# Hybrid decoder block on one core: modulation product moved to TensorE, state-space quarters and indexer blocks woven in another order

## The chip, the cores and the metric

One core of a Trainium2 chip runs the whole kernel in one launch. The metric is the device time in microseconds (us), and lower is better. Engines are named as in the profile: PE is TensorE, PEld its weight loads, DVE VectorE, ACT ScalarE, POOL GpSimd, SPq the queue of DMA issues on SyncE and ACTq that on ScalarE.

## The reference

One layer on 512 tokens of width 1024, all float32:

```python
ada = silu(c) @ w_ada + b_ada                       # 1024 -> 6144: shift1, scale1, gate1, shift2, scale2, gate2
u = rms_norm(h, norm1_g) * (1 + scale1) + shift1
u_ssm, q, k, v, q_idx, k_idx, w_idx, g_ssm, g_attn = split(u @ w_in)
y_ssm  = s5_mixer(u_ssm)                            # 32 groups, state 64, complex diagonal scan, GLU
y_attn = dsa_attention(q, k, v, q_idx, k_idx, w_idx)
mixed = sigmoid(g_ssm) * (y_ssm @ w_proj_ssm) + sigmoid(g_attn) * (y_attn @ w_proj_attn)
h = h + gate1 * (mixed @ w_out)
u2 = rms_norm(h, norm2_g) * (1 + scale2) + shift2
h = h + gate2 * moe_ffn(u2)                         # 64 experts, top 8, and a shared one
out = rms_norm(h, norm_f)
# dsa_attention, per block of 128 queries:
score = sum over 8 heads of w_idx * relu(q_idx @ k_idx.T); sel = top_k(causal(score), 128)
p = softmax(q @ k[sel].T / 8 - slope * distance); y = p @ v[sel]
```

## The kernel before, in words

Each engine runs a program written out by hand, and semaphores tie them together. PSUM results ("groups") go to banks in the order of the list `groups_in_order()`: a group takes bank `ORDER[g] % NB`, and PE waits until the group `NB` places earlier was copied out, by DVE for the kinds in `BY_VECTOR` and else by ACT. Weights stream through three slots of 2 MB in the order of `stream_items()`; SyncE issues them in that order, each when the item three places earlier is no longer used, so one late item holds all behind it. The items ("A", n) are the twelve 2 MB pieces of `w_ada`; four pieces make one part of 2048 outputs.

The stages, in order of time:

- Start. `ada_piece(0)` to `(3)` on DVE multiply and add a piece into the 128-partition accumulator `ADA` (L1069, two instructions of 128x2048 a piece). Between the pieces DVE makes the norm's factor. PE transposes the scaled rows of x (`uT`, L1501) and sums `ADA` over the partitions (`mod`, L1608), and DVE and ACT scale `uT` by the result (L1104, L900). Only then can `ssm`, the first projection, start.
- Projections `ssm`, `kkT`, `vwT`, `qiT` on PE (L1521), with small transposes `cT` between them.
- State space and indexer. The 32 groups of the state space are worked in four quarters q. POOL builds the tables of a quarter (`s5_tables(q)`: BA, then CA, then W2; L591, L666, L673, L684). `s5_build(q)` on PE makes bT and K of BA and CA, DVE's `s5_kernel(q)` makes a Toeplitz kernel of K. `s5_apply(q)` on PE: u chunks (`uc`), v1 and v2 (L1572, L1578), a gate projection `gs`, and y (L1591 to L1593), for which DVE must have ended `s5_scan(q)` (L1121 to L1134) and POOL W2(q). `s5_phases(q)` on DVE makes the next scan's angles. The key indexer of block i: eight head products `idx` (256, 384 and 512 keys wide for i = 1, 2, 3), a relu copy by ACT into two buffers in turn, and a multiply-add over the heads by DVE (`index_scores(i)`, L1153). `top_k(i)` on DVE takes the 8 largest 16 times (L1161, L1162).
- Projection `qT`, then four attention blocks i of 8 heads: logits (PE), bias and maximum (DVE, L1225 to L1227), exp (ACT), transpose and product with v (PE). Eight gate projections stand in them at the places `FILL`. `top_k(3)` stands in blocks 0 and 1, `top_k(2)` ahead of block 0, and half a piece of `w_ada` on DVE two heads behind each of the eight fills.
- GLU, the sums of `ADA` over the partitions (`ada`, n = 4 to 11), branches, output projection, routing and 43 passes of the experts. Their code is the same in both kernels.

## Time and profile before

| | |
|---|---|
| runs of the kernel before | 1324.74, 1328.32, 1328.75 us; median 1328.32 |
| the profiled execution | 1327.42 us, its span 1325.7 us |
| first projection starts | 53.40 us |
| projection qT starts | 265.51 us |
| first logits of attention block 1, 2, 3 | 326.8, 356.9, 391.8 us |
| attention ends on PE | 426.3 us |

The engines' shares of the whole span (PE 88%, DVE 43%, POOL 20%) are averages over stages with different limits, so the table gives the borders of the stages that the change touches. Everything behind 426 us waits for what comes before it in one chain.

### The profile page before, as it was taken

To read this page: it belongs to the slowest core of one execution; us is meant where nothing else is said; L and a number is where in the kernel's file an instruction comes from. 1 tells how busy PE (TensorE), PEld (TensorE's weight loads), DVE (VectorE), ACT (ScalarE), POOL (GpSimd) and SP (SyncE) were. 2 spreads that over 40 slices of the span, in tenths; PEclk is the share of its full clock that TensorE was granted. 3 is DMA by queue.
4 is the path that set the end of the run, shared out by engine and by line. 5 is a ranking of instruction groups with operands and counts; after the bars stand their busy time and mean duration, and the time that the engine had idled before them with its cause. 6 is when DMAs were issued, how large, how long until landed. Compare 5 with 4: busy or idle time off the path is not lost. (4 is left out here: it accounts for less than half of the span.)

```text
span 1325.7 us, 13190 instructions
## 1 busy us (share of the span) xinstructions
PE 1166.0 (88%) x4654; PEld 569.8 (43%) x4655; DVE 566.9 (43%) x1175; ACT 226.8 (17%) x449; POOL 260.1 (20%) x250
## 2 busy tenths in 40 slices
PE   0799677797999999989789999999998999999854
PEld 0544455544555444444433444444444444444321
DVE  5325989877744412343722232222222222232138
ACT  2411231123324000111001111111111111111111
POOL 7852478200000000001001111111111111111100
PEclk9799787898899999999889999999999999999977
DMA  8726100331213212220969999999999899899776
GB/s 324 187 87 206 26 9 10 97 147 84 109 83 140 83 64 79 80 83 6 376 262 347 422 419 394 362 379 416 385 413 421 339 383 401 344 420 376 268 315 264
DMA packets 84902, 318.37 MB, mean 240 GB/s; under 512 B 29842, under 2 KB 32914, under 8 KB 56162
## 3 DMA queue, kind: packets, MB, share of 16 engines
q1 hardware_dynamic: 64084, 277.96, 53.6%
q0 software_dynamic: 14352, 36.23, 7.2%
q10 hardware_dynamic: 6400, 3.33, 1.1%
q8 instruction: 38, 0.62, 0.2%
q14 instruction: 28, 0.23, 0.0%
HBM read 302.14 MB, written 29.89 MB: 250 GB/s over the span
## 5 line engine op out<-in xcount | busy, mean ns | idle before, releaser
L1521 PE MATMUL ps<-uTs,ring 128*128 128x512 f32 (+2 forms) x496 | 228.4, 619 | 3.3 <-DMA ring<-in_w_in 2.6
L1789 PE MATMUL ps<-ring,XT 128*128 128x512 f32 x416 | 183.0, 593 | 0.4 <-ACT XT L998 0.4
L1822 PE MATMUL ps<-ring,XT 128*64 128x512 f32 (+1 forms) x800 | 148.8, 595 | 0.9 <-ACT XT L998 0.9
L1521 PEld LDWEIGHTS ps<-uTs,ring 128*128 128x128 f32 (+2 forms) x496 | 95.6, 196 | 122.7 <-issue 118.2
L1383 DVE TENSOR_TENSOR uTs<-uTs,ps 128x256 f32<-128x256 f32 x47 | 19.8, 421 | 283.5 <-ACT uTs L1002 283.5
L738 POOL DMA_INDIRECT XT<-u_rows,idx x48 | 49.0, 1021 | 409.0 <-DVE idx L1372 387.0
L1789 PEld LDWEIGHTS ps<-ring,XT 128*128 128x128 f32 x416 | 77.2, 191 | 87.8 <-issue 87.2
L1833 PE MATMUL ps<-ring,uTs 128*128 128x512 f32 x208 | 98.8, 619 | 3.2 <-DMA ring<-in_w_exp_down 3.1
L1424 DVE TENSOR_SCALAR uTs<-ps,gat 128x512 f32<-128x512 f32 x47 | 35.3, 751 | 128.3 <-PE ps L1833 70.1
L1822 PEld LDWEIGHTS ps<-ring,XT 128*64 128x64 f32 (+1 forms) x800 | 46.4, 128 | 87.4 <-issue 84.1
L1852 PE MATMUL ps<-ring,uTs 128*64 128x512 f32 (+1 forms) x400 | 80.2, 626 | 1.8 <-DMA ring<-in_w_exp_down 1.7
L1501 PEld LDWEIGHTS ps<-ident,XT 128*128 128x128 f32 x424 | 53.1, 189 | 53.3 <-DMA XT<-u_rows,idx 38.6
L1501 PE MATMUL ps<-ident,XT 128*128 128x128 f32 x424 | 60.6, 288 | 16.5 <-DMA XT<-u_rows,idx 10.3
L744 POOL DMA_INDIRECT expert_rows<-uTs,adx x47 | 47.5, 1011 | 139.7 <-DVE uTs L1424 139.7
L591 POOL TENSOR_TENSOR ring<-ring 128x512 f32<-128x512 f32 (+4 forms) x35 | 56.9, 1625 | 79.0 <-issue 28.0
L1069 DVE SCALAR_TENSOR_TENSOR ADA<-ring,sm,ADA 128x2048 f32<-128x2048 f32 x24 | 60.1, 2506 | 27.9 <-DMA ring<-in_w_ada 14.2
L1002 ACT ACTIVATE uTs<-ps 128x256 f32<-128x256 f32 x47 | 18.1, 384 | 310.2 <-PE ps L1789 169.9
L712 POOL DMA_DIRECT2D u_rows<-XT x4 | 2.4, 612 | 326.9 <-DVE XT L1266 326.9
L1007 ACT ACTIVATE uTs<-ps,gat 128x512 f32<-128x512 f32 x47 | 32.3, 688 | 162.6 <-PE ps L1833 87.7
L1833 PEld LDWEIGHTS ps<-ring,uTs 128*128 128x128 f32 x208 | 38.4, 195 | 42.5 <-issue 42.2
L1521 PE MATMUL ps<-ring,UB 128*128 128x512 f32 x128 | 55.4, 593 | 1.5 <-DVE UB L1253 1.5
L836 ACT ACTIVATE ring<-ps 128x512 f32<-128x512 f32 (+3 forms) x60 | 29.5, 505 | 117.1 <-PE ps L1521 106.6
(319 smaller groups left out, 1377.9 us busy)
## 6 DMA issues: line engine op xcount, KB each, us to landing
ring<-in_w_exp_gate SPq DMA_DIRECT2D x64, 1024.0 KB, 10.5
ring<-in_w_exp_up SPq DMA_DIRECT2D x64, 1024.0 KB, 15.0
ring<-in_w_exp_down SPq DMA_DIRECT2D x64, 1024.0 KB, 14.7
ring<-in_w_ada SPq DMA_DIRECT2D x12, 2048.0 KB, 12.2
ring<-in_w_in SPq DMA_DIRECT2D x7, 2048.0 KB, 9.0
ring<-expert_rows SPq DMA_DIRECT2D x6, 2048.0 KB, 18.6
ring<-in_w_out SPq DMA_DIRECT2D x2, 2048.0 KB, 8.7
H<-in_x SPq DMA_DIRECT2D x1, 2048.0 KB, 14.1
```

The costliest lines, as they stand in the source:

```text
L591: link(E.tensor_tensor(o, x, y, op))
L738: E.indirect_dma_start(xg[par], None, U2D, bass.IndirectOffsetOnAxis(idx[:, col:col + 1], 0), bounds_check=SEQ - 1, oob_is_err=False).then ...
L744: E.indirect_dma_start(YD, bass.IndirectOffsetOnAxis(adx[:, col:col + 1], 0), y, None, bounds_check=SEQ * EK - 1, oob_is_err=False).then_i ...
L1007: A(ye[p % 2][:, 512:1024], ps[7][:, :], ACT.Copy, scale=gat[:, p % RING:p % RING + 1]).then_inc(S["y_out_s"], 1)
L1069: return V.scalar_tensor_tensor(acc, a3(arrived(dve, ("A", n)), 2)[:, k], csil[:, 2 * j + k:2 * j + k + 1], acc, ALU.mult, ALU.add)
L1424: V.tensor_scalar(ye[p % 2][:, 0:512], ps[6][:, :], gat[:, p % RING:p % RING + 1], None, ALU.mult)\
L1501: return nc.tensor.transpose(o, i, ident[0:k, 0:k])
L1521: ins = mm(b[0:rows_, 0:cols], l, r, start=(k == 0), stop=(k == len(chunks) - 1))
L1789: ins = mm(a3(ps[0][:, :], 2), xgT[par][:, k], wgu[r][:, k], start=(k == 0), stop=(k == KD - 1))
L1822: ins = mm(a3(ps[0][c, :], 2), xgT[par][:, k, c], wgu[r][:, k], start=(k == 0), stop=(k == KD - 1))
L1833: ins = mm(ps[6 + n][:, :], hTe[:, k], a3(wdn[r], 2)[:, k, 512 * n:512 * (n + 1)], start=(k == 0), stop=(k == 1))
L1852: ins = mm(ps[6 + n][c, :], hTe[:, k, c], a3(wdn[r], 2)[:, k, 512 * n:512 * (n + 1)], start=(k == 0), stop=(k == 1))
```

## The change

1. `w_ada` on PE: `ada_piece(n)` takes a column of silu(c), repeated to 32 columns, as the weights, and writes four quarters of 512 outputs to the four groups of 32 partitions of bank 5, which it keeps (`NB` is 5). `ada_row(part)` on DVE adds the bias once a part. The `mod` product becomes four transposes, and `ada` picks its row with a column of the identity. x is loaded ahead of `w_ada`.
2. `s5_build(0)`, `uc` of quarter 0 stand among the `qiT` projections; quarter 0 is applied ahead of every indexer block; then indexer block i stands ahead of `s5_apply(i)`, i = 1, 2, 3, and `s5_build(q + 1)` inside `s5_apply(q)`.
3. `top_k(1)` stands behind the last scan, `top_k(2)` in attention block 0 and `top_k(3)` in block 1, two rounds a head.

```diff
@@ -44,7 +44,7 @@
-NB = 6
+NB = 5
...
-        return [("uc", q), ("v1", q), ("v2", q), ("gs", q)] + [("y", q, n) for n in range(2)]
+        return [("v1", q), ("v2", q), ("gs", q)] + (s5_build(q + 1) if q + 1 < NQ else []) + [("y", q, n) for n in range(2)]
+
+    def indexer(i):
+        return [("idx", i, h) for h in range(NH - 2)] + [("uc", i)] + [("idx", i, h) for h in range(NH - 2, NH)]
-    o += [("kkT", 0), ("vwT", 0), ("vw", 0)] + [("qiT", m) for m in range(4)]
-    o += [("idx", 1, h) for h in range(NH)] + s5_build(0)
-    o += [("idx", 2, h) for h in range(NH)] + s5_apply(0) + s5_build(1)
-    o += [("idx", 3, h) for h in range(NH)] + s5_apply(1) + s5_build(2)
-    o += s5_apply(2) + s5_build(3) + s5_apply(3)
+    o += [("kkT", 0), ("vwT", 0), ("vw", 0), ("qiT", 0), ("qiT", 1)] + s5_build(0)
+    o += [("qiT", 2), ("uc", 0), ("qiT", 3)] + s5_apply(0)
+    for i in range(1, TT):
+        o += indexer(i) + s5_apply(i)
...
+        ada_rows = [ADA[:, 2048:2560], ADA[:, 4096:4608], ADA[:, 4608:5120]]
...
+            sp.dma_start(H[:], a["x"][0].rearrange("(t p) d -> p t d", p=P)).then_inc(S["x_in"], 16)
+
+            def bias_of_part(part):
+                for q in range(4):
+                    c0 = 2048 * part + 512 * q
+                    sp.dma_start(ada_rows[part][32 * q:32 * (q + 1), :], a["b_ada"][0:1, c0:c0 + 512].broadcast_to((32, 512)))\
+                        .then_inc(b_in[part], 16)
+
             load(("A", 0))
-            sp.dma_start(H[:], a["x"][0].rearrange("(t p) d -> p t d", p=P)).then_inc(S["x_in"], 16)
             load(("A", 1))
-            for n, c in enumerate((slice(0, 2 * DM), slice(2 * DM, 6 * DM))):
-                sp.wait_ge(S["ada_zero"], n + 1)
-                sp.dma_start(ADA[0:1, c], a["b_ada"][0:1, c]).then_inc(b_in[n], 16)
+            bias_of_part(0)
             for g in list(ITEMS)[2:]:
                 if g == ("misc", 0):
                     state_tables()
-                if g == ("A", 5):
+                    bias_of_part(1)
+                    bias_of_part(2)
+                if g == ("gs", 0):
...
+            s5_tables(2)
             causal(1)
+            s5_tables(3)
             causal(2)
-            s5_tables(2)
             causal(3)
-            s5_tables(3)
...
+                    if h == NH - 2:
+                        chunks(i)
...
-            for m in range(4):
+            for m in range(2):
                 out_copy(("qiT", m), qiT[:, m, :])
             phases(0)
-            indexer(1)
             arrange_u(0)
             s5_build(0)
-            indexer(2)
+            out_copy(("qiT", 2), qiT[:, 2, :])
+            chunks(0)
+            out_copy(("qiT", 3), qiT[:, 3, :])
             s5_apply(0)
-            phases(1)
-            s5_build(1)
-            indexer(3)
-            s5_apply(1)
-            phases(2)
-            s5_build(2)
-            s5_apply(2)
-            phases(3)
-            s5_build(3)
-            s5_apply(3)
+            for q in range(1, NQ):
+                phases(q)
+                indexer(q)
+                s5_apply(q)
...
-            V.memset(ADA[:, 0:2 * DM], 0.0).then_inc(S["ada_zero"], 1)
-            V.memset(ADA[:, 2 * DM:6 * DM], 0.0).then_inc(S["ada_zero"], 1)
-
-            dve.wait_ge(b_in[0], 16)
-            dve.wait_ge(S["c_silu"], 1)
-
-            def ada_half(n, k):
-                part, j = n // 4, n % 4
-                acc = ADA[:, 2048 * part:2048 * (part + 1)]
-                return V.scalar_tensor_tensor(acc, a3(arrived(dve, ("A", n)), 2)[:, k], csil[:, 2 * j + k:2 * j + k + 1], acc,
-                                              ALU.mult, ALU.add)
-
-            def ada_piece(n):
-                link(ada_half(n, 0))
-                signal(ada_half(n, 1), "ada_sum", n + 1)
+            def ada_row(part):
+
+                dve.wait_ge(b_in[part], 64)
+                dve.wait_ge(S["ada_sum"], 4 * (part + 1))
+                V.tensor_tensor(ada_rows[part], ada_rows[part], ps[5][:, :], ALU.add).then_inc(S["ada_row"], 1)
...
-            for n in range(2):
-                ada_piece(n)
             dve.wait_ge(S["squares"], 1)
             rms_scale(slice(0, TT), 1)
             V.tensor_copy(junk1, rstd[:, 0:1]).then_inc(S["rstd_ok"], 1)
-            for n in range(2, 4):
-                ada_piece(n)
+            ada_row(0)
...
-            dve.wait_ge(b_in[1], 16)
             dve.wait_ge(S["scan_zero"], 1)
-            ada_piece(4)
             taken(dve, ("vw", 0))
             link(V.tensor_scalar(wis, vw[:, :, HD:HD + NH], float(NH * 64) ** -0.5, None, ALU.mult))
             s5_phases(0)
-            ada_piece(5)
-            index_scores(1)
             s5_kernel(0)
-            index_scores(2)
-            s5_scan(0)
-            s5_phases(1)
-            s5_kernel(1)
-            index_scores(3)
-            s5_scan(1)
-            s5_phases(2)
-            s5_kernel(2)
-            ada_piece(6)
-            s5_scan(2)
-            s5_phases(3)
-            top_k(1, 0, 4)
-            s5_kernel(3)
-            top_k(1, 4, 10)
-            s5_scan(3)
-            top_k(1, 10, 16)
-            ada_piece(7)
-            top_k(2, 0, 16)
+            for q in range(NQ):
+                s5_scan(q)
+                if q + 1 < NQ:
+                    s5_phases(q + 1)
+                    s5_kernel(q + 1)
+                    index_scores(q + 1)
+            top_k(1, 0, 16)
+            ada_row(1)
...
-                        top_k(3, n, n + 1)
+                    if i < 2:
+                        top_k(2 + i, 2 * h, 2 * h + 2)
...
-                    if (i, h - 2) in FILL:
-                        k = list(FILL).index((i, h - 2))
-                        if k % 2 == 0:
-                            link(ada_half(8 + k // 2, 0))
-                        else:
-                            signal(ada_half(8 + k // 2, 1), "ada_sum", 9 + k // 2)
...
+            ada_row(2)
             for n in range(4, 12):
+                if n == 9:
+                    done(dve, ("ada", 11))
                 ada_out(n)
...
+            def ada_piece(n):
+
+                part, j = n // 4, n % 4
+                w = a3(arrived(pe, ("A", n)), 2)
+                if n == 0:
+                    pe.wait_ge(S["c_silu"], 1)
+                elif j == 0:
+                    pe.wait_ge(S["ada_row"], part)
+                for k in range(2):
+                    col = csil[:, 2 * j + k:2 * j + k + 1].broadcast_to((P, 32))
+                    for q in range(4):
+                        ins = mm(ps[5][32 * q:32 * (q + 1), :], col, w[:, k, 512 * q:512 * (q + 1)],
+                                 start=(j == 0 and k == 0), stop=(j == 3 and k == 1))
+                ins.then_inc(S["ada_sum"], 1)
+
             def ada(n):
-                pe.wait_ge(S["ada_sum"], 4 * (n // 4 + 1))
-                end(product(("ada", n), [(ones[:], ADA[:, 512 * n:512 * (n + 1)])]))
+                pe.wait_ge(S["ada_row"], n // 4 + 1)
+                row = ident[:, 32 * (n % 4):32 * (n % 4) + 1].broadcast_to((P, P))
+                end(product(("ada", n), [(row, ada_rows[n // 4])]))
...
+            def s5_apply(q):
+                if 1 <= q < 3:
+                    ada_piece(4 + q)
...
+                if q + 1 < NQ:
+                    s5_build(q + 1)
...
                 for h in range(NH):
+                    if h == NH - 2:
+                        chunks(i)
...
+            ada_piece(0)
+            ada_piece(1)
             for t in range(TT):
                 pe.wait_ge(S["u_tile"], t + 1)
                 transposed_rows("uT", t, ut4)
-            pe.wait_ge(S["ada_sum"], 4)
+            ada_piece(2)
+            ada_piece(3)
+            pe.wait_ge(S["ada_row"], 1)
             b = begin(("mod", 0))
-            for c in range(2 * KD):
-                ins = mm(b[:, c:c + 1], ADA[:, P * c:P * (c + 1)], ones[:, 0:1], start=True, stop=True)
+            for c in range(4):
+                ins = tr(b[:, P * c:P * (c + 1)], ada_rows[0][:, P * c:P * (c + 1)])
...
-            pe.wait_ge(S["u_ok_v"], KD // 2)
-            pe.wait_ge(S["u_ok_s"], KD // 2)
             w = a3(arrived(pe, ("ssm", 0)), 8)
             for t in range(TT):
-                end(product(("ssm", t), [(uT[:, k, P * t:P * (t + 1)], w[:, k]) for k in range(KD)]))
+                b = begin(("ssm", t))
+                for k in range(KD):
+                    if t == 0:
+                        pe.wait_ge(S["u_ok_s" if k % 2 else "u_ok_v"], k // 2 + 1)
+                    ins = mm(b[:, :], uT[:, k, P * t:P * (t + 1)], w[:, k], start=(k == 0), stop=(k == KD - 1))
+                end(ins)
...
-            for m in range(4):
+            for m in range(2):
                 projection_t("qiT", m, w, P * m)
-            taken(pe, ("qiT", 3))
+            s5_build(0)
+            projection_t("qiT", 2, w, P * 2)
+            chunks(0)
+            projection_t("qiT", 3, w, P * 3)
...
-            indexer(1)
-            s5_build(0)
-            indexer(2)
+            ada_piece(4)
             s5_apply(0)
-            s5_build(1)
-            indexer(3)
-            s5_apply(1)
-            s5_build(2)
-            s5_apply(2)
-            s5_build(3)
-            s5_apply(3)
+            taken(pe, ("qiT", 3))
+            for q in range(1, NQ):
+                indexer(q)
+                s5_apply(q)
             w = a3(arrived(pe, ("q", 0)), 8)
             for m in range(4):
                 projection_t("qT", m, w, P * m)
+            ada_piece(7)
...
+                        if list(FILL).index((i, h)) % 2:
+                            ada_piece(8 + list(FILL).index((i, h)) // 2)
```

On ACT the helper `chunks(q)` (the copy of `uc` and the arranging of the next quarter's chunks) is cut out of `s5_apply` in the same way.

PE at the start, before: the transposes of the rows of x (`UB`), the product `mod` and the first projection.

```order
L1501 MATMUL ps<-ident,K16s 128x32 x2
L1501 MATMUL ps<-ident,UB 128x128 x32
L1608 MATMUL ps<-ones,ADA 128x1 x16
L1521 MATMUL ps<-ring,uTs 128x512 x32
L1501 MATMUL ps<-ident,XT 128x128 x8
```

The same place after (`ring,sm 32x512` is a piece of `w_ada`, 8 products each):

```order
L1482 MATMUL ps<-ident,K16s 128x32 x2
L1521 MATMUL ps<-ring,sm 32x512 x16
L1482 MATMUL ps<-ident,UB 128x128 x32
L1521 MATMUL ps<-ring,sm 32x512 x16
L1482 MATMUL ps<-ident,ADA 128x128 x4
L1625 MATMUL ps<-ring,uTs 128x512 x32
```

Two pieces now stand on each side of the transposes, and four transposes in the place of sixteen products.

DVE from the last angle of quarter 0 to its scan, before (`score` rows are the indexer's, `ADA` a piece of `w_ada`, `K16s` the Toeplitz kernel, L1121 the scan's first instruction):

```order
L1069 SCALAR_TENSOR_TENSOR ADA<-ring,sm,ADA 128x2048 x2
L1151 TENSOR_SCALAR score<-GB,sm 128x256
L1153 SCALAR_TENSOR_TENSOR score<-GB,sm,score 128x256 x7
L1111 TENSOR_TENSOR sm<-ident,sm 16x128
L1115 COPY K16s<-ps 16x4x112
L1116 TENSOR_TENSOR K16s<-ps,sm 16x4x16
L1115 COPY K16s<-ps 16x4x112
L1116 TENSOR_TENSOR K16s<-ps,sm 16x4x16
L1151 TENSOR_SCALAR score<-GB,sm 128x384
L1153 SCALAR_TENSOR_TENSOR score<-GB,sm,score 128x384 x7
L1121 TENSOR_SCALAR ring<-ring,sm 128x512
```

DVE after, from the kernel of quarter 1 to its scan:

```order
L1109 TENSOR_TENSOR sm<-ident,sm 16x128
L1113 COPY K16s<-ps 16x4x112
L1114 TENSOR_TENSOR K16s<-ps,sm 16x4x16
L1113 COPY K16s<-ps 16x4x112
L1114 TENSOR_TENSOR K16s<-ps,sm 16x4x16
L1149 TENSOR_SCALAR score<-GB,sm 128x256
L1151 SCALAR_TENSOR_TENSOR score<-GB,sm,score 128x256 x7
L1119 TENSOR_SCALAR ring<-ring,sm 128x512
```

Two indexer blocks stood ahead of the scan of quarter 0; now the first of them stands between the kernel of quarter 1 and its scan.

DVE in attention block 0, before (one head; `score` 128x512 is a round of `top_k(3)`):

```order
L1161 MAX sm<-score 128x8
L1162 MATCH_REPLACE score<-sm,score 128x512
L1225 SCALAR_TENSOR_TENSOR ring<-ps,ring 128x128
L1226 TENSOR_REDUCE sm<-ring 128x1
L1227 TENSOR_SCALAR sm<-sm 128x1
```

After, ahead of the same head:

```order
L1159 MAX sm<-score 128x8
L1160 MATCH_REPLACE score<-sm,score 128x384
L1159 MAX sm<-score 128x8
L1160 MATCH_REPLACE score<-sm,score 128x384
L1209 SCALAR_TENSOR_TENSOR ring<-ps,ring 128x128
```

A head carries two rounds in the place of one, 384 wide in block 0 and 512 wide in block 1.

## Rows read from the trace of the kernel before

**Rows 1.** Engines by stretch: us, busy time with (x instructions), PE clock, DMA share, GB/s

```profile
0.00:53.40 53.40, 13.34 (x67) 12.95 (x68) 28.90 (x25) 24.27 (x37) 38.15 (x58) 0.89 0.81 261
53.40:127.20 73.80, 73.12 (x172) 31.61 (x172) 24.77 (x27) 7.55 (x13) 36.98 (x26) 0.96 0.48 151
127.20:265.50 138.30, 101.19 (x625) 73.51 (x624) 123.37 (x172) 34.20 (x85) 78.11 (x53) 0.83 0.16 46
...
295.00:326.80 31.80, 23.93 (x80) 12.73 (x78) 23.84 (x56) 13.11 (x34) 0.00 (x0) 0.84 0.31 129
326.80:356.90 30.10, 27.56 (x102) 15.21 (x101) 23.80 (x51) 8.77 (x27) 0.00 (x0) 0.89 0.06 14
356.90:391.80 34.90, 33.28 (x127) 19.46 (x126) 16.39 (x30) 10.82 (x27) 0.00 (x0) 0.85 0.42 170
391.80:426.30 34.50, 32.72 (x150) 19.32 (x149) 17.60 (x29) 13.52 (x28) 0.00 (x0) 1.00 0.23 84
```

**Rows 2.** Timeline of DVE and PE at the start: start, us, what [idle before]

```profile
20.62 10.37 DVE L1069 SCALAR_TENSOR_TENSOR ADA<-ring,sm,ADA 128x2048 f32<-128x2048 f32 x4 [13.28 <-DMA ADA<-in_b_ada]
...
32.73 10.00 DVE L1069 SCALAR_TENSOR_TENSOR ADA<-ring,sm,ADA 128x2048 f32<-128x2048 f32 x4
...
42.79 6.99 PE L1608 MATMUL ps<-ones,ADA 128*128 128x1 f32 x32 [2.78 <-DVE ADA L1069]
53.40 30.57 PE L1521 MATMUL ps<-ring,uTs 128*128 128x512 f32 x64 [3.62 <-issue]
```

**Rows 3.** Loads: SyncE issues, first use of x, GB/s in 40 slices of 0 to 40 us

```profile
7.65 18.54 SPq L424 DMA_DIRECT2D ring<-in_w_ada  x2
...
15.80 1.06 ACT L825 ACTIVATE UB<-H 128x1024 f32<-128x1024 f32 x1 [4.01 <-DMA H<-in_x]
...
GB/s 0 10 109 270 394 385 409 426 274 139 346 394 410 426 426 422 402 393 410 394 402 418 418 443 328 25 82 197 393 434 401 434 281 348 410 406 408 378 153 28
```

**Rows 4.** Timeline of DVE, index_scores(1), (2) and (3) without their first instruction

```profile
129.68 3.61 DVE L1153 SCALAR_TENSOR_TENSOR score<-GB,sm,score 128x256 f32<-128x256 f32 x7
...
136.97 13.22 DVE L1153 SCALAR_TENSOR_TENSOR score<-GB,sm,score 128x384 f32<-128x384 f32 x7
...
172.60 12.33 DVE L1153 SCALAR_TENSOR_TENSOR score<-GB,sm,score 128x512 f32<-128x512 f32 x7
```

**Rows 5.** As rows 1: W2(1); BA, CA(2); scans 1, 2, 3; y(1); v1 to y(0) with build(1); build(0)

```profile
167.70:175.20 7.50, 6.29 (x42) 3.60 (x40) 5.09 (x7) 4.18 (x8) 7.14 (x5) 1.00 0.00 0
176.60:194.70 18.10, 13.74 (x64) 8.73 (x64) 17.75 (x13) 3.18 (x5) 17.37 (x11) 0.72 0.12 17
184.90:195.20 10.30, 9.87 (x48) 4.88 (x44) 10.05 (x11) 0.40 (x1) 9.31 (x7) 0.81 0.12 17
213.50:226.80 13.30, 8.49 (x20) 3.46 (x16) 13.05 (x10) 0.60 (x1) 12.83 (x7) 0.88 0.06 9
251.70:257.30 5.60, 4.70 (x11) 1.72 (x10) 5.35 (x11) 0.60 (x1) 0.00 (x0) 1.00 0.11 17
195.20:200.70 5.50, 5.43 (x49) 5.26 (x49) 5.19 (x11) 0.96 (x5) 0.00 (x0) 1.00 0.00 0
...
148.30:169.60 21.30, 21.22 (x136) 15.98 (x136) 15.79 (x28) 5.03 (x14) 4.45 (x4) 0.85 0.10 15
130.20:133.10 2.90, 2.90 (x27) 2.30 (x26) 2.72 (x6) 2.35 (x6) 0.00 (x0) 1.00 1.01 429
```

**Rows 6.** Timeline: SyncE issues w_in of q behind the last gs; PE begins qT

```profile
256.43 0.37 SPq L427 DMA_DIRECT2D ring<-in_w_in  x1
...
265.51 27.73 PE L1521 MATMUL ps<-uTs,ring 128*128 128x512 f32 x64 [2.63 <-DMA ring<-in_w_in]
```

**Rows 7.** Groups by form: busy us, mean ns | idle before; 32-column tiles, rounds of top_k(3)

```profile
L1852 PE MATMUL ps<-ring,uTs 128*32 128x512 f32 x128 | 16.3, 653 | 0.1
...
L1161 DVE MAX8 sm<-score 128x8 f32<-128x512 f32 x16 | 11.0, 686 | 0.1
L1162 DVE MATCH_REPLACE8 score<-sm,score 128x512 f32<-128x512 f32 x16 | 10.8, 676 | 0.0
```

19 lines of the change are left out of this document (11 added, 8 removed).

## The prediction, made before the changed kernel ran

> **What bounds the kernel now.** I read the engines by stretch first [rows 1]. Behind 426 us both kernels run the same code in one chain, so I take a microsecond saved or lost ahead of that point as a microsecond of the whole. Ahead of it the stages have different limits. From 0 to 53.4 us PE is busy 13.3 us: it waits for the modulation. From 53.4 to 127.2 it is busy 73.1 of 73.8, so the projections are PE's. From 127.2 to 265.5 PE has 101 of 138 us and DVE 123 of 138: DVE's order of work bounds the state space. In attention blocks 0 and 1 PE and DVE share the bound (24 and 24 of 31.8 us; 28 and 24 of 30.1), and blocks 2 and 3 are almost PE's (33.3 of 34.9, 32.7 of 34.5).
>
> At the start DVE first touches a piece of w_ada at 20.6 us, held by the bias row, and has 20.4 us of such work ahead of mod, which costs PE another 7.0; the first projection follows at 53.4 [rows 2]. The loads are no limit there for long: the GB/s row adds up to 2.1, 4.2, 6.3 and 8.4 MB at about 8, 14.5, 20 and 25 us and then falls to 25 GB/s, because SyncE issues the fourth piece only when DVE has used the first, at 26.2 us (7.65 + 18.54) [rows 3].
>
> In the state space index_scores costs 0.52 us an instruction (3.61 / 7) while GpSimd rests, but 1.89 and 1.76 us (13.22 / 7, 12.33 / 7) while it builds tables [rows 4]. A scan takes 10.3 and 13.3 us beside tables and 5.6 without [rows 5]. So the two engines slow each other down, or rather DVE pays, and where a block stands against the tables matters more than its length.
>
> **Term 1, the start.** Removed from the path: DVE's 20.4 us and mod's 7.0. x is now the first load, so it lands near 9 us and not at the 15.8 of [rows 3], and norm and transposes hide behind the pieces. PE takes piece 0 at about 15 and frees its slot by 17, while loads are still queued; the dip at 25 us goes. At 410 GB/s, with 0.3 MB of bias, piece 3 is in by 31 and the weights of ssm by 36. A piece on PE is 8 float32 products of two instructions on 32 columns. The nearest row has 128 such instructions in 16.3 us, 0.127 us each [rows 7], so 16 make 2.0 us, and up to 4.0 at half clock. Piece 3 ends at 34, the bias add and four transposes take an estimated 1.5, and of the 3.6 us between mod's end and the first projection (42.79 + 6.99 to 53.40 [rows 2]) I keep 1.5, as PE now waits chunk by chunk. T0, the start of ssm, is 37: a gain of 16.4, from 12 (the norm's gain vector or the angles late) to 18.
>
> The Trainium skill, TensorEngine Tiling (Array Packing), section Key Properties, lets tiles work in parallel but says that changing the tiling mode drains the engine. That speaks against pieces of 2 us strewn among full-width products. The row above comes from passes that stand between full-width products, so it already holds such changes, and I add nothing for it.
>
> **Term 2, from T0 to qT.** Before: 265.5 - 53.4 = 212.1. After, in PE's order: the projections 73.8 [rows 1], build(0) 2.9, uc an estimated 0.7, piece 4 2.0, then v1, v2, gs, build(1) and y(0), which are the 21.3 us of [rows 5]: y(0) ends at T0 + 100.7. DVE's scan 0 hides beside gs, since GpSimd rests then. Three quarters follow.
> - Quarter 1. GpSimd starts with W2(1), 7.5, when y(0) is out, then BA and CA of quarter 2, 18.1 [rows 5], which build(2) needs; with K (an estimated 1.9) and y(1), 5.5, that makes 33.0. DVE's way is as long: 2 until the first relu, eight instructions, scan 12, y 5.5. The block is 256 wide, and its own row says 0.52; beside tables I take 1.6, from the 1.76 and 1.89, so 12.8 and together 32.3. I take 33.
> - Quarter 2. DVE works without a pause: phases and kernel 9.6 (11 of the 13 phases' instructions take 5.2 [rows 5]), index 15 (8 x 1.89), scan 12 (between 10.3 and 13.3). I take 36.6.
> - Quarter 3. Only W2(3) is left, so about three of the eight instructions are slow. uc is out 12 us behind y(2), v1, v2 and gs take 12.5, and q's weights arrive 9.1 us behind gs (265.51 - 256.43 [rows 6]): 33.6.
>
> Pieces 5 and 6, 2.0 each, stand where PE waits for DVE; without that cover they would cost 4. SyncE issues eight bias loads more ahead of misc, which is needed a whole ssm (30.57 us [rows 2]) later, and the chunk loads now ahead of gs: nothing.
>
> Sum: 100.7 + 33 + 36.6 + 33.6 = 203.9, a gain of 8.2. Bounds: GpSimd's 33.0 holds in quarters 1 and 2 even if DVE were quick, so the gain is at most 14 here; with 1.89 everywhere and scans of 13.3 it falls to 2, and a stall of a few us a quarter makes it a loss of 4. Against the 256 row alone quarter 1 would be no shorter, but phases(2) would start earlier: 2.4 us more gain.
>
> The Trainium skill, GPSIMD Engine Reference, section Key points, says that GpSimd shares its SBUF interfaces with VectorE and contends with its instructions of two SBUF inputs. By that the 256 block, moved from a rest of GpSimd into its tables, becomes slow, and top_k, moved out, gains nothing; the 384 and 512 rows agree, and no row here shows the 256 block under tables.
>
> **Term 3, attention.** top_k(1) stands beside qT (27.7 us of PE) and is hidden there. Piece 7 behind qT meets ACT's table loads and gelu; bounds 0 and 2, I take 1. A round of top_k on 512 keys is 0.686 + 0.676 and the small load and gaps, 1.5 us [rows 7]; on 384 an estimated 1.25. Block 0: eight rounds of 512 (12) become sixteen of 384 (20), and two halves of a piece leave (2 x 2.3 estimated): DVE goes from 23.8 to 27.2 us of 31.8, and PE with piece 8 from 23.9 to 26. It fits, as DVE can run two heads ahead inside a fill: 0. Block 1: sixteen rounds of 512 for eight, less two halves, is 23.8 + 12 - 4.7 = 31.1 us in a block of 30.1. If all its waits vanish it costs 1, if they stay (6.3) it costs 7.3; walking the heads through the two fills gives 3.7, which I take. Blocks 2 and 3 are PE's: pieces 10 and 11 cost 2.0 each. Sum: a loss of 8.7, from 4 to 14.
>
> **Term 4, behind GLU.** ada_row(2) comes after DVE's product with the gate, just when PE reaches the sums of the third part: a loss of 1, from 0 to 3. Five banks in the place of six: a projection lasts 6.9 us and its copy well under 1, so I put it at nothing in the projections, and inside the walk above in attention.
>
> **Sum.** -16.4 - 8.2 + 8.7 + 1 = -14.9. The profiled execution took 1327.4 us, of which 1325.7 are its span; the median of the runs is 0.9 above it. 1327.4 - 14.9 + 0.9 gives 1313 us.
>
> **Rivals.**
> - Less contention (0.12): tables and DVE miss each other, term 2 gains 14 and block 1 costs 1. For it: GpSimd is idle 60 of the stage's 138 us [rows 1]. Against: the index block now starts just when W2 does. 1304 or a little under.
> - Attention bounded by DVE (0.12): block 1 pays 7.3 and block 0 some 4, as the fills leave DVE without logits. 1321.
> - Loads late at the start (0.06): piece 3 or the small loads behind 10 MB land 6 us later. For it: the bias row, issued at 3 us, held DVE until 20.6. 1319.
> - The new order stalls (0.07): a relu buffer holds uc, uc holds v1 and ca_ok holds build by turns, 5 to 6 us a quarter. Term 2 becomes a loss of about 8: 1329, no difference to slightly slower.
> - Slower (0.05): the four tiles of a piece don't overlap, so a piece costs 16 x 0.433 = 6.9 us (27.73 / 64 [rows 6]). Each of the five pieces 7 to 11 then costs 4.9 more on PE, in blocks with no room: +25, 1338. It ends the gain when a piece takes about 5 us. Against it stands the 0.127 of [rows 7], whose moving data is the same shape.
>
> **How the numbers follow.** The forecast holds 0.58, with its own range 1305 to 1320. From 1300 to 1326 lie it, the first three rivals and some of the fourth. A measurement of this kernel tells about 0.3%, 4 us, from no change, so faster means under 1324: 0.58 + 0.12 + 0.12 + 0.05 = 0.87, from which I take 0.01 for the tails. Within 4 us 0.07, slower 0.07.
>
> **What would show it.** Piece products near 2 us; ssm at 35 to 40 us, and no dip in the GB/s at 25; y(0) about 101 us behind ssm; W2(1) starting with y(0)'s copy and the 256 block at about 1.6 us an instruction; qT near 241; block 0 as long as before, block 1 about 4 longer, 2 and 3 about 2 longer; the same time behind attention. I am wrong if PE's first projection is still held past 45 us, if a quarter takes over 40 us, or if block 1 passes 38.

## The result, and the profile after

The changed kernel took 1318.57 us (median of 8 runs, 1314.11 to 1322.73) against 1327.06 us before (8 runs, 1324.74 to 1329.89). The ratio is 0.9936, with a 95% interval of 0.992 to 0.9953: 8.5 us faster, where 14 were forecast. The execution that was profiled is the quickest of the eight (1314.11 us, span 1312.4). From the start of the output projection on (522.42 us after, 531.40 before), where both kernels run the same code, it takes 4.3 us less than the one before; at that border it is 9.0 us ahead, and this is the part that answers to the medians.

Engines by stretch, the changed kernel: us, busy time with (x instructions) of PE, PEld, DVE, ACT, POOL, then PE clock, DMA share, GB/s. The borders are the first projection, the end of y(0), the starts of index blocks 2 and 3 (one quarter each), qT, the first logits of blocks 0 to 3, GLU and the output projection.

```profile
0.00:38.59 38.59, 16.86 (x102) 7.32 (x103) 4.25 (x16) 24.09 (x37) 22.43 (x52) 0.98 0.93 338
38.59:138.99 100.40, 96.88 (x356) 48.24 (x357) 28.76 (x56) 15.38 (x29) 51.34 (x42) 0.97 0.50 152
138.99:172.60 33.61, 28.31 (x177) 17.85 (x176) 30.36 (x32) 8.39 (x23) 22.99 (x15) 0.85 0.07 9
172.60:206.70 34.10, 28.68 (x178) 18.41 (x176) 30.85 (x36) 9.12 (x23) 24.66 (x16) 0.90 0.06 9
206.70:238.72 32.02, 25.44 (x138) 16.61 (x136) 28.10 (x60) 8.95 (x24) 10.32 (x12) 0.84 0.29 88
238.72:271.84 33.12, 33.12 (x112) 15.17 (x113) 5.19 (x16) 5.54 (x6) 0.31 (x1) 0.95 0.38 142
271.84:305.34 33.50, 27.29 (x92) 13.39 (x90) 26.48 (x78) 11.25 (x33) 0.00 (x0) 0.85 0.24 99
305.34:340.81 35.47, 29.33 (x118) 15.50 (x117) 29.23 (x70) 8.88 (x27) 0.00 (x0) 0.90 0.10 31
340.81:378.00 37.19, 35.54 (x141) 19.68 (x140) 11.77 (x28) 10.81 (x27) 0.00 (x0) 0.86 0.35 141
378.00:416.26 38.26, 36.48 (x166) 20.51 (x165) 13.09 (x27) 13.47 (x28) 0.00 (x0) 0.96 0.27 95
416.26:522.42 106.16, 104.19 (x246) 45.60 (x246) 27.18 (x39) 9.53 (x12) 0.00 (x0) 1.00 0.23 80
```

Blocks 0 to 3 answer to the last four rows of [rows 1]. qT was this row of the same view in the kernel before:

```profile
265.51:295.08 29.57, 29.57 (x95) 13.98 (x95) 23.40 (x50) 3.58 (x5) 0.21 (x1) 1.00 0.32 116
```

Taken together, stretch by stretch:

| stretch | before | after | difference | forecast |
|---|---|---|---|---|
| start to the first projection | 53.40 | 38.59 | -14.8 | -16.4 |
| first projection to qT | 212.1 | 200.1 | -12.0 | -8.2 |
| qT to the end of attention | 160.75 | 177.54 | +16.8 | +8.7 |
| GLU to the output projection | 105.1 | 106.2 | +1.0 | +1.0 |
| sum | | | -9.0 | -14.9 |

Timeline of PE at the start: start, us, what, and in brackets the idle time before it with what ended it. It answers to [rows 2].

```profile
15.54 3.64 PE L1521 MATMUL ps<-ring,sm 128*32 128x512 f32 x16 [6.85 <-DMA ring<-in_w_ada]
20.99 3.64 PE L1521 MATMUL ps<-ring,sm 128*32 128x512 f32 x16 [1.81 <-DMA ring<-in_w_ada]
...
29.32 1.92 PE L1521 MATMUL ps<-ring,sm 128*32 128x512 f32 x16
32.05 1.92 PE L1521 MATMUL ps<-ring,sm 128*32 128x512 f32 x16 [0.81 <-DMA ring<-in_w_ada]
34.86 0.66 PE L1482 MATMUL ps<-ident,ADA 128*128 128x128 f32 x4 [0.89 <-DVE ADA L1074]
38.59 21.80 PE L1625 MATMUL ps<-ring,uTs 128*128 128x512 f32 x44 [3.07 <-DMA ring<-in_w_in]
```

A piece takes 3.64 us at the lower clock and 1.92 at the full one, and each of the idle times but one ends with a load (DMA share 0.93 in the first stretch).

Timeline of PE in attention block 1, the changed kernel:

```profile
307.93 0.44 PE L1482 MATMUL ps<-ident,ring 128*128 128x128 f32 x2 [1.46 <-ACT ring L954]
311.93 0.69 PE L1482 MATMUL ps<-ident,ring 128*128 128x128 f32 x2 [2.94 <-ACT ring L954]
312.42 9.32 PE L1502 MATMUL ps<-uTs,ring 128*128 128x512 f32 x16
...
329.09 0.44 PE L1482 MATMUL ps<-ident,ring 128*128 128x128 f32 x2 [1.74 <-ACT ring L954]
```

Before the two fills, 2.94 and 1.74 us of idle stand where there were 0.66 and 0.22: ACT's exp is named, but it waits for DVE's maximum, and that stands behind two rounds of the selection. Three things went into the 16.8 us. PE's idle time (length less busy) is 15.8 us for 13.8, so 2.0 more. The time at half clock, (1 - clock) x 2 x length in each row, is 33.9 us for 27.3. It costs something only where PE is busy, and half of its length there: read in steps of 0.25 us, PE was busy in 31.1 of the 33.9 us and in 22.2 of the 27.3 (in block 0 of the kernel before, 3.4 us of it fell on idle PE). That makes 4.5 us. Five pieces of 2.05 us each, a price that e4 takes apart, make 10.2. Together that is 16.7.

### The profile page after: what moved, and what is told of

Its sections match the earlier page's. It is cut to its first block and busy times, and to the rows that moved or that the text cites. A ratio compares the mean times of both kernels' runs of the same rounds, so it can differ in the third digit from the quotient of the medians.

```text
span 1312.4 us, 13490 instructions
## 1 busy us (share of the span) xinstructions
PE 1186.5 (90%) x4818; PEld 561.9 (43%) x4819; DVE 493.8 (38%) x1152; ACT 226.9 (17%) x449; POOL 238.5 (18%) x250
## 5 line engine op out<-in xcount | busy, mean ns | idle before, releaser
L1502 PE MATMUL ps<-uTs,ring 128*128 128x512 f32 (+2 forms) x496 | 234.0, 631 | 3.1 <-DMA ring<-in_w_in 2.5
L1364 DVE TENSOR_TENSOR uTs<-uTs,ps 128x256 f32<-128x256 f32 x47 | 19.8, 421 | 284.9 <-ACT uTs L1012 284.9
L1482 PEld LDWEIGHTS ps<-ident,XT 128*128 128x128 f32 x424 | 52.9, 189 | 49.1 <-DMA XT<-u_rows,idx 36.6
L601 POOL TENSOR_TENSOR ring<-ring 128x512 f32<-128x512 f32 (+4 forms) x35 | 48.7, 1391 | 73.1 <-ACT UB L899 40.3
L1502 PE MATMUL ps<-XT,ring 128*128 128x512 f32 x96 | 42.7, 593 | 0.0
## 6 DMA issues: line engine op xcount, KB each, us to landing
ring<-in_w_exp_gate SPq DMA_DIRECT2D x64, 1024.0 KB, 10.7
```

The source lines that it names most:

```text
L601: link(E.tensor_tensor(o, x, y, op))
L1482: return nc.tensor.transpose(o, i, ident[0:k, 0:k])
L1502: ins = mm(b[0:rows_, 0:cols], l, r, start=(k == 0), stop=(k == len(chunks) - 1))
```

## Experiments

Theory A, at the start of the study: some 8 of attention's 16.8 us come from the selections in blocks 0 and 1 (waits, and the lower clock behind waits), and the rest from pieces that cost 1.92 us each where PE is the bound. Rival B: the loss is the pieces, the fifth bank and the clock, whatever DVE does.

**e1: selections beside qT again**

```diff
             top_k(1, 0, 16)
+            top_k(2, 0, 16)
             ada_row(1)
...
                     if i < 2:
-                        top_k(2 + i, 2 * h, 2 * h + 2)
+                        top_k(3, n, n + 1)
```

> The changed kernel with one thing undone: the selection for query block 2 (16 rounds) stands beside the q projection again, behind that for block 1, and attention blocks 0 and 1 hold one round a head of block 3's selection. Theory A: of the 16.7 us that the stretch from the q projection to the end of attention lost, the selections in blocks 0 and 1 made some 8: the waits for VectorE and, behind them, fills at the lower clock. Then block 1 falls from 35.5 to about 32, the stretch ahead of block 1 from 37.3 to about 35, and the kernel is 5 to 9 us quicker than the changed one (about 1312). Theory B: the loss is the pieces' own time on TensorE, the fifth bank and the clock, whatever VectorE does. Then the kernel stays within 2 us of the changed one (about 1318).

It took 1307.70 us (1306.81 to 1309.17; ratio to before 0.9864, interval 0.985 to 0.9879): 10.9 us less than the changed kernel (9.9 if each is set against the kernel before of its own session, 1326.09 and 1327.06), somewhat over A's range. Engines by stretch, qT and blocks 0 to 3:

```profile
240.04:273.29 33.25, 33.25 (x113) 15.12 (x113) 23.26 (x61) 5.55 (x6) 0.03 (x1) 0.95 0.37 139
273.29:304.21 30.92, 25.71 (x92) 12.84 (x90) 17.68 (x51) 11.17 (x33) 0.00 (x0) 0.89 0.26 107
304.21:337.07 32.86, 29.76 (x117) 15.64 (x116) 19.09 (x49) 8.88 (x27) 0.00 (x0) 0.90 0.10 33
337.07:369.42 32.35, 30.71 (x142) 17.09 (x141) 11.71 (x28) 10.70 (x27) 0.00 (x0) 1.00 0.40 163
369.42:407.67 38.25, 36.47 (x166) 20.52 (x165) 13.09 (x27) 13.47 (x28) 0.00 (x0) 0.96 0.27 97
```

DVE's 18 us of selection vanish beside qT (its busy time there goes from 5.2 to 23.3 us, the stretch stays at 33). The attention is 9.9 us shorter: 2.6 in each of blocks 0 and 1, and 4.8 in block 2, where no selection was. Block 2 has the same instructions and the same idle time as in the changed kernel, but a clock of 1.00 for 0.86. The rival is out: the selections in blocks 0 and 1 cost the kernel some 10 us by the medians. By the profiles 5.2 of them stand in those two blocks; whether the 4.8 of block 2 come from the selections is not shown (see the part on the prediction).

**e2: part 1 alone.** The kernel before with all of part 1 (pieces on PE, x first, five banks) and nothing of parts 2 and 3. Cut to the places of pieces 4 to 6; piece 7 stands behind qT, 8 to 11 in attention as in the changed kernel.

```diff
             def s5_apply(q):
+                if 1 <= q < 3:
+                    ada_piece(4 + q)
...
                 projection_t("qiT", m, w, P * m)
+            ada_piece(4)
```

> The kernel before with the modulation product on TensorE alone (x loaded first, five banks, bias by parts), with the old order of the state space and the old places of the selections; pieces 4 to 7 stand on TensorE before the index blocks, ahead of uc of quarters 1 and 2, and behind the q projection. Theory A: the start gives 14.8, and VectorE, relieved of pieces 4 to 7 (some 4.7 us each) and bound in the state space, gives 8 to 12 more ahead of the q projection even in the old order; attention loses some 5 to 8 for the pieces. Sum about 1327 - 14.8 - 10 + 6 = 1308. Theory B: the gain of 12.0 ahead of the q projection comes from the new order of quarters and index blocks. Then this kernel gains the start alone and pays attention's pieces: about 1327 - 14.8 + 6 = 1318.

1318.41 us (1317.37 to 1321.26; ratio 0.9949, 0.9936 to 0.9963), the time of the whole change. The first projection starts at 39.21, qT at 247.69: ahead of qT 208.5 us, a gain of 3.6, not A's 8 to 12. Attention takes 169.9 us, 9.1 more than before. Theory B of this run holds. With e1 the three parts come apart. Each median is set against the kernel before of its own session: e2 -7.7, e1 -18.4, the changed kernel -8.5.

| step | kernels | us |
|---|---|---|
| part 1, product on PE | e2 less before | -7.7 |
| part 2, new order of quarters and index blocks | e1 less e2 | -10.7 |
| part 3, selections into attention | changed less e1 | +9.9 |

The third part gave back what the second had brought. By the profiles, 4.9 of the 10.7 us and 4.8 of the 9.9 stand in block 2 of attention (37.25 us in e2, 32.35 in e1, 37.19 in the changed kernel) and go with its clock.

**e3 and e7: why a piece takes 1.92 us**

```diff
-                for k in range(2):
-                    for q in range(4):
+                for q in range(4):
+                    for k in range(2):
```

> The changed kernel with the two loops of a piece exchanged: both products of one group of 32 output rows follow each other, then those of the next group, so neighbours mostly write the same rows. If products on different 32-column groups run beside each other only when they are neighbours, most of the overlap goes: a piece takes from 1.92 us up to 5 to 6.9 us (16 x 0.433), the four in attention and piece 7 cost 3 to 4.9 us more each, the start some 5 more: 1338 to 1350. If the short time of a piece does not come from that overlap, a piece stays near 1.9 us and the time within 2 us of the changed kernel.

1318.39 us (1316.56 to 1320.94), pieces of 1.94 us: the order in which the four groups are written makes no difference. This left two explanations, and e7 tells them apart (pieces n with n % 4 > 0 write only the first 32 rows, so the modulation's values are wrong, the count of products is the same; the flags that open and close the sums are set to match):

```diff
-                        ins = mm(ps[5][32 * q:32 * (q + 1), :], col, ...)
+                        r = q if j == 0 else 0
+                        ins = mm(ps[5][32 * r:32 * (r + 1), :], col, ...)
```

> The changed kernel with all eight products of pieces 1 to 3, 5 to 7 and 9 to 11 sent to the first group of 32 output rows (the modulation is then wrong in value; same count and shape of products). Theory A: a piece takes 1.92 us because products on four groups run beside each other, each group with its own queue deep enough that their order in the program doesn't matter. On one group they can't: a piece takes 6.9 us (16 x 0.433), five of pieces 7 and 9 to 11 and those at the start cost some 5 us each: 1338 to 1348. Theory B: a product on 32 columns is short by itself (0.12 us), with or without neighbours: 1318, a piece 1.9 us.

Timeline of PE in block 1 of e7:

```profile
350.53 7.05 PE L1522 MATMUL ps<-ring,sm 128*32 128x512 f32 x16
```

7.05 us for 16 instructions on one group: a product on 32 columns is as long as a full one, and the 1.92 us are four groups at work beside each other. The price of the forecast's rival (6.9 us a piece) was right, its condition wasn't met. Attention is 15.7 us longer than in the changed kernel and the start 13.0. The whole, 1418.19 us, can't be compared: other modulation chooses other experts.

The Trainium skill, TensorEngine Tiling (Array Packing), section Key Properties, says that tiles run their matrix products in parallel, and these two runs agree. It names no condition on their order; of the two orders tried within 16 instructions, both overlap.

**e4: pieces 8 to 11 all but out** (one product of 32 columns in the place of eight; the modulation's third part is incomplete).

```diff
-                    for q in range(4):
+                    for q in range(4 if n < 8 else 0):
...
+                if n >= 8:
+                    ins = mm(ps[5][0:32, 0:32], col, w[:, 0, 0:32], start=(j == 0), stop=(j == 3))
```

> The changed kernel with pieces 8 to 11, the four that stand in attention, cut from eight products to one of 32 columns each (the third part of the modulation is then incomplete). Theory A: TensorE is the bound in blocks 2 and 3 and ahead of block 1, so these pieces cost their 1.92 us there; in block 1 about half: 6 to 8 us quicker in all, about 1311.5. Theory B: behind the waits for VectorE a piece of TensorE is free, and the loss is waits and clock: 0 to 3 us quicker.

1305.97 us (1305.16 to 1309.83), 12.6 less than the changed kernel, more than either theory gave. Behind attention the two profiles take the same 896 us, so the incomplete modulation doesn't disturb the comparison. Engines by stretch, blocks 2 and 3:

```profile
341.80:372.47 30.67, 29.03 (x127) 16.81 (x126) 11.71 (x28) 10.70 (x27) 0.00 (x0) 1.00 0.48 194
372.47:407.36 34.89, 33.11 (x152) 19.39 (x151) 13.09 (x27) 13.47 (x28) 0.00 (x0) 1.00 0.24 87
```

Block 3 now has the clock of 1.00 that it had before, and takes 34.89 us where it took 34.51: the tiny product on 32 columns costs nearly 0.4. Timeline of PE in block 3, from its second fill to the logits behind it: the kernel before, e4, and the changed kernel.

```profile
409.91 7.03 PE L1521 MATMUL ps<-uTs,ring 128*128 128x512 f32 x16
...
417.71 1.12 PE L1521 MATMUL ps<-kT,XT 64*128 64x512 f32 x2
```

```profile
390.63 7.03 PE L1502 MATMUL ps<-uTs,ring 128*128 128x512 f32 x16
397.59 0.25 PE L1525 MATMUL ps<-ring,sm 128*32 128x32 f32 x2
...
398.80 1.12 PE L1502 MATMUL ps<-kT,XT 64*128 64x512 f32 x2
```

```profile
397.85 7.03 PE L1502 MATMUL ps<-uTs,ring 128*128 128x512 f32 x16
...
407.70 1.12 PE L1502 MATMUL ps<-kT,XT 64*128 64x512 f32 x2
```

From start to start that is 7.80, 8.17 and 9.85 us. The tiny product itself takes 0.18 to the next instruction (397.59 to 397.77), so the two changes of shape, from full width to 32 columns and back, cost 0.2 us, and a whole piece costs 9.85 - 7.80 = 2.05 us, close to the 2.0 of the forecast. The Trainium skill, TensorEngine Tiling (Array Packing), section Key Properties, has changes of the tiling mode drain the engine; a price like this would fit, but nothing here measures the drain by itself. The block's 38.26 us are then 34.51 + 2.05 + 1.7, the last for its 3.4 us at half clock (the first fill takes 8.35 us and not 7.03). In block 2 e4 is at full clock and the changed kernel isn't: 6.5 us between them, though e4 keeps the selections in blocks 0 and 1.

**e5: pieces where PE waits anyway.** e1, with pieces 8, 9 and 11 ahead of the wait for the block's first weights.

```diff
                     n = NH * i + h
+                    if h == 0 and i != 2:
+                        ada_piece({0: 8, 1: 9, 3: 11}[i])
                     pe.wait_ge(S["prob"], n + 1)
...
-                        if list(FILL).index((i, h)) % 2:
-                            ada_piece(8 + list(FILL).index((i, h)) // 2)
+                        if (i, h) == (2, 5):
+                            ada_piece(10)
```

> The kernel of e1 with pieces 8, 9 and 11 moved from behind the second fill of attention blocks 0, 1 and 3 to the head of the block, ahead of the wait for the first weights of the block (2.30, 1.46 and 1.78 us of idle TensorE in e1). Theory A: a piece costs its 1.92 us only where TensorE has no wait to lay it in, and part of what it adds is a spell at half clock. Then the three pieces cost under 1 us each: 4 to 7 us quicker than e1, about 1302; block 3 falls from 38.3 to about 35. Theory B: the place doesn't matter, since the wait moves behind the piece or the piece delays the block's own chain: within 2 us of e1 (1307.7).

1297.18 us (1293.34 to 1302.68; ratio to before 0.978, 0.9756 to 0.9804), 10.5 less than e1 and over A's range. Engines by stretch, blocks 0 to 3 of e5 (qT, 33.12 us at a clock of 0.95, is as in e1):

```profile
271.81:300.25 28.44, 24.41 (x91) 12.14 (x89) 17.68 (x51) 11.06 (x33) 0.00 (x0) 0.94 0.28 116
300.25:328.52 28.27, 26.74 (x118) 14.57 (x117) 19.10 (x49) 8.77 (x27) 0.00 (x0) 1.00 0.05 14
328.52:360.86 32.34, 30.70 (x141) 17.09 (x140) 11.70 (x28) 10.70 (x27) 0.00 (x0) 1.00 0.46 184
360.86:395.38 34.52, 34.52 (x166) 19.76 (x165) 13.09 (x27) 13.47 (x28) 0.00 (x0) 1.00 0.24 85
```

The profiled execution is e5's quickest (1293.34 us). The same work as e1 on PE, 10.9 us shorter in attention: idle time 7.2 us for 11.7, and 6.7 us at half clock for 19.8, which at half price is 6.5; both sum to 11.1. Block 3 is the plainest, and 34.52 us in all three kernels with piece 11 at its head (e5, e9, e12). In e1 PE waited 1.78 us and then ran its fill at the lower clock; in e5 the piece stands in the wait, no idle time is left in the block and the fill takes 7.03 us:

```profile
373.18 1.07 PE L1483 MATMUL ps<-ident,ring 128*128 128x128 f32 x4 [1.78 <-ACT ring L954]
374.04 8.35 PE L1503 MATMUL ps<-uTs,ring 128*128 128x512 f32 x16
```

```profile
362.77 1.92 PE L1522 MATMUL ps<-ring,sm 128*32 128x512 f32 x16
365.12 7.03 PE L1503 MATMUL ps<-uTs,ring 128*128 128x512 f32 x16
```

The first fence is e1, the second e5.

**e12: the same places, selections left in attention.** The changed kernel with e5's edit.

> The changed kernel, selections left in attention blocks 0 and 1, with pieces 8, 9 and 11 at the heads of blocks 0, 1 and 3. Theory A: the pieces' price (their time and the spells at half clock behind the waits at the heads) and VectorE's waits inside blocks 0 and 1 are apart: 8 to 10 us quicker than the changed kernel, about 1309.5, block 3 at 34.5 and block 1 still with its waits of 2.9 and 1.7. Theory B: with VectorE behind, the piece at the head of blocks 0 and 1 is no gain; only block 3's 3.7 us come: about 1314.5.

1312.35 us (1307.62 to 1315.38; ratio 0.9893, 0.9877 to 0.991), 6.2 less than the changed kernel and between the two theories. Engines by stretch, blocks 0, 1 and 3:

```profile
272.66:304.51 31.85, 27.06 (x91) 13.20 (x90) 26.48 (x78) 11.18 (x33) 0.00 (x0) 0.84 0.25 103
304.51:339.71 35.20, 30.13 (x117) 15.74 (x116) 29.24 (x70) 8.65 (x27) 0.00 (x0) 0.90 0.04 12
...
376.59:411.11 34.52, 34.52 (x166) 19.75 (x165) 13.10 (x27) 13.47 (x28) 0.00 (x0) 1.00 0.23 84
```

Block 3 gives its 3.7 us, block 0 gives 1.7, block 1 next to nothing (35.20 for 35.47; its waits ahead of the fills are 2.62 and 2.25 us for 2.94 and 1.74): while DVE sets its length, a piece laid into one wait comes back in another.

**e6, e9: GpSimd's order.** e1 with W2(q) behind BA and CA of q + 1; e9 is e5 with the same.

```diff
...
             s5_tables(0)
+            s5_w2(0)
             s5_tables(1)
             s5_tables(2)
+            s5_w2(1)
             causal(1)
             s5_tables(3)
+            s5_w2(2)
+            s5_w2(3)
             causal(2)
```

> The kernel of e1 with one thing moved on GpSimd: W2(q) (7.5 us) behind BA and CA of quarter q+1 and not ahead of them. Theory A: GpSimd's 33 us from one y to the next bound quarters 1 and 2, because build(q+1) waits 3.96 and 2.88 us for CA. With W2 behind, the table comes 7.5 us earlier and W2 is first needed by y: its floor is 25.6 + 5.5 = 31.1 us. Then the waits for CA go, the two quarters take 31 to 32.5 us instead of 33.7 and 34.1, and the kernel is 2 to 4 us quicker than e1, about 1304.5. Theory B: VectorE's row of phases, kernel, index scores and scan bounds the quarters and the wait for CA only covers for it: within 1 us of e1.

1305.83 us (1300.25 to 1307.69), 1.9 less than e1. Timeline of PE, changed kernel, the waits for CA (POOL L683), of which e6 has none:

```profile
164.14 3.21 PE L1555 MATMUL ps<-ring 128*16 128x128 f32 x16 [3.96 <-POOL ring L683]
...
199.56 1.92 PE L1555 MATMUL ps<-XT,ring 128*16 128x128 f32 x16 [2.88 <-POOL XT L683]
```

And e6 by quarters:

```profile
138.60:172.20 33.60, 28.93 (x178) 18.47 (x177) 29.57 (x32) 8.27 (x23) 23.88 (x16) 0.85 0.07 10
172.20:206.30 34.10, 30.08 (x178) 18.73 (x177) 31.56 (x36) 9.13 (x23) 24.25 (x15) 0.85 0.06 9
```

The waits are gone, and the two quarters (33.6 and 34.1 us, DVE busy 29.6 and 31.6 of them) are as long as in the changed kernel: the wait for CA had mostly covered one for DVE. So far B holds, but not to the end. In e1 itself the two quarters took 32.4 and 36.6, and seven kernels with the same code ahead of qT, but for the order of the loads in e8 and within a piece in e3 (the changed one, e1, e3, e4, e5, e8, e12) need 200.1 to 202.6 us from the first projection to qT. e6 needs 199.2 and e9 199.5. The new order of GpSimd may thus be worth about 1 us, less than A said; such a difference is within the scatter of these kernels and not shown.

> e5 and e6 together: selection for block 2 beside the q projection, pieces 8, 9 and 11 at block heads, W2(q) behind BA and CA of q+1. Theory A: e5 took 10.5 us from e1 in attention and e6 1.9 ahead of it, in different stretches, so they add: about 1295.5. Theory B: e6's 1.9 us is the scatter of the state space from kernel to kernel (from y(0) to y(3) 96 to 100 us among kernels with the same order there): the same as e5, 1297.

1293.77 us (1288.97 to 1300.9; ratio 0.9756, 0.9731 to 0.9781): the fastest version, 32.4 us less than the kernel before in the same session (1326.12). That it beats e5 is not certain, since the two intervals overlap. Its profiled execution needs 199.5 us from the first projection to qT, e5's 200.1. In attention the two have the same code and agree in blocks 1 to 3, but block 0 took 32.59 us at a clock of 0.79 in e9 and 28.44 at 0.94 in e5: a piece at the head of that block doesn't always spare it the lower clock.

**e10, e11: VectorE relieved, meant to be.** Seven of eight index score instructions of a block on 64 keys (the scores are incomplete); e10 is the changed kernel with this, e11 is e6.

```diff
-V.scalar_tensor_tensor(sc_of[i], relu[:, n % 2, 0:w], wcol, sc_of[i], ALU.mult, ALU.add)
+V.scalar_tensor_tensor(sc_of[i][:, 0:64], relu[:, n % 2, 0:64], wcol, sc_of[i][:, 0:64], ALU.mult, ALU.add)
```

> The changed kernel with seven of the eight index score instructions of each block on 64 keys and not on 256, 384 or 512 (the scores are then incomplete; the selection reads other data at the same cost). It takes some 11, 8 and 7 us from VectorE in quarters 1, 2 and 3. Theory A, the forecast's step: GpSimd's W2(1), BA and CA of the next quarter, K and y, 33.0 us, bound quarters 1 and 2 even if VectorE is quick. Then y(0) to y(1) stays at 33 and y(1) to y(2) goes to about 33 from 34.1; the kernel gains at most some 3 us ahead of the q projection. Theory B: VectorE's row bounds them and GpSimd is itself slowed by VectorE. Then they fall to 28 or less, GpSimd's tables get shorter too, and the q projection starts 8 to 15 us earlier.

> e6 (W2 behind the tables) with the same narrow index scores. Theory A: with VectorE relieved, GpSimd's order is worth what its floor says, 33.0 against 31.1 us a quarter: 4 us earlier at the q projection than e10. Theory B: no difference to e10, GpSimd bounds neither.

Neither tells the theories apart, because the edit took next to nothing from DVE in quarter 1. Timeline of DVE, the changed kernel:

```profile
142.20 12.13 DVE L1151 SCALAR_TENSOR_TENSOR score<-GB,sm,score 128x256 f32<-128x256 f32 x7
...
210.17 7.08 DVE L1151 SCALAR_TENSOR_TENSOR score<-GB,sm,score 128x512 f32<-128x512 f32 x5
```

and e10, where the last row stands behind GpSimd's tables of the quarter:

```profile
143.93 11.56 DVE L1151 SCALAR_TENSOR_TENSOR score<-GB,sm,score 128x64 f32<-128x64 f32 x7
...
216.51 0.28 DVE L1151 SCALAR_TENSOR_TENSOR score<-GB,sm,score 128x64 f32<-128x64 f32 x1 [0.79 <-ACT GB L846]
```

A quarter of the width, 1.65 us for 1.73. With GpSimd at rest the same instruction takes 0.28. In quarters 2 and 3 the seven instructions took 7.5 and 5.9 us for 9.65 and 8.62, so DVE was relieved by 2 to 3 us there and not by the 8 and 7 that the runs were meant to take. qT starts at 238.37 (e10) and 236.47 (e11) for 238.72. The medians (1337.64 of 2 runs and 1329.26 us) are not comparable, as the selections and through them the experts change.

**e8: load order.** The changed kernel with x behind piece 0.

> The changed kernel with x loaded behind piece 0 of w_ada, as before, and not ahead of it. Theory A: the start is bound by the loads of 10 MB and of the projection's weights, so the order in which the first two come makes no difference to the projection: it starts within 1 us of 38.6. Theory B: norm and transposes are on the path, and x 5 us later puts them behind piece 3: the first projection starts 2 to 5 us later and the kernel is as much slower, about 1322.

1318.67 us (1316.94 to 1321.68), the first projection at 38.16: no difference, A holds. That x comes first is worth nothing. That the bytes bound the start is argued, from the DMA share of 0.93 and the waits for loads; no run took bytes away.

## Why the prediction was right, and where it wasn't

The direction held, and with it the mechanism of the gain (the start and the state space). The time lies in the range, 5.6 us above the forecast, and that owes something to luck: term 3 lost 8.1 us more than forecast, and term 2 happened to give 3.8 more. Without that the kernel would have stood near 1322, outside the forecast's own range. By the forecast's own terms:

- **Term 1**, 16.4 forecast, 14.8 measured. The pieces' price (2.0 us, 4.0 at half clock) was 1.92 and 3.64, and piece 3 ended at 34.0 as forecast. The 1.6 us lie behind it: the weights of ssm were expected by 36 and ended PE's wait at 38.6. The credit for x as the first load was wrong in its cause (e8).
- **Term 2**, 8.2 forecast, 12.0 measured. y(0) came 100.4 us behind the first projection, for 100.7. The quarters took 33.6, 34.1 and 32.0 for 33, 36.6 and 33.6. This profile is at the quick end: seven kernels with nearly this code need 200.1 to 202.6 us from the first projection to qT (e6). The 256-wide block took 1.73 us an instruction for the 1.6 assumed. The 384- and 512-wide ones cost less than the 1.89 taken for all, 9.65 / 7 = 1.38 and 8.62 / 7 = 1.23: five of the 384-wide ones ran beside W2's instructions of 1.3 to 1.6 us (6.46 / 5 = 1.29), and the last two of 512 behind the tables (1.54 / 2 = 0.77). The step "GpSimd's 33.0 holds in quarters 1 and 2 even if DVE were quick" stays untested: e6 shows only that DVE's way is about as long, and e10 and e11 did not make DVE quick. It was a bound of the range and moved the forecast little.
- **Term 3**, a loss of 8.7 forecast and 16.8 measured, is the step that failed. The price of a piece was right (2.05 us for 2.0), and so was block 2's loss (2.3). Wrong was where PE has slack, and at which clock it works. "It fits: 0" for block 0 and 1 for piece 7 overlooked that PE's slack in a block stands at its waits and not where the piece stood: qT with piece 7 cost 3.6 (1.92 and some 1.6 for half clock) and block 0 1.8, with 2.6 us that the selections cost there (e1) against fewer waits elsewhere. Block 1 cost 5.4, between the 3.7 taken and the 7.3 of the rival. Block 3 cost 3.7 for 2.0, of which 1.7 is the clock. The forecast priced every microsecond of PE at the clock of the old row, but the lower clock alone took 4.5 of the 16.8 us. The bounds, 4 to 14, were too narrow for the same reason.
- **Term 4**, 1.0 as forecast. Five banks were not compared with six in a run of their own; e5, with five, has block 3 without any idle time of PE, so none for a bank.

The rival "attention bounded by DVE" (1321) named a mechanism that was there, at about half of its size (2.6 us each in blocks 0 and 1 by e1, for 7.3 and some 4), and the median lies between it and the forecast. What no case had was the clock: 4.8 of e1's 9.9 us stand in block 2, which holds no selection.

The cause of that stays open. In the changed kernel, e1 and e5 less idle time goes with less time at half clock (33.9, 19.8 and 6.7 us), but e6, with e1's idle times in attention, spends some 27 us at half clock there. Block 2 is at a clock of 1.00 in e1, e4, e5, e9 and e11, and at 0.85 or 0.86 in the kernel before, the changed one, e2, e3, e6, e8, e10 and e12. Two of these speak against the selections as the cause: e6 has e1's code from qT on and needs 37.24 us for the block, and e4 keeps the selections in blocks 0 and 1 and needs 30.67. Clock rows of block 2 (us, PE busy, PE clock, DMA share, GB/s), first the changed kernel, then e1, both behind a wait of 1.62 us at the block's head:

```profile
344.00:346.00 2.00, 2.00 (x5) 0.58 0.98 410
346.00:348.00 2.00, 2.00 (x11) 0.50 1.03 430
```

```profile
342.00:344.00 2.00, 2.00 (x15) 1.00 1.01 422
```

The wait is the same, the clock isn't. What went before differs: block 1 with waits of 1.46, 2.94 and 1.74 us in the one, of 1.46, 1.42 and 0.22 in the other. Yet e2 and e6 have the idle times of block 1 as in e1 and block 2 at 0.86. So which wait the clock answers to stays open, and how much of the 4.8 us the selections caused.

## What to carry to other kernels

An engine's slack counts only at the place where it waits: a piece of 2 us cost 2.3 and 3.7 us behind a fill in blocks 2 and 3 (1.7 of the last for the clock) and nothing at the head of block 3, where PE waited for its first weights, and the same 18 us of selection cost some 10 us by the medians inside attention and nothing beside a projection that DVE sat out. Before work is moved into a stage, walk its waits one by one, not its sum of busy and idle time. When a large change gives little, time its parts alone: here one part gave back what another had brought, and the undone kernel (e1) with better places for the pieces (e5) is 30 us faster than before and not 8.5.
